# Background copies and additions of weight sums, each behind a finished panel of its own

## The reference, cut to what matters

```
h = layer_norm(ALPHA * h + mix, g, b)
h = layer_norm(ALPHA * h + square(relu(h @ w1)) @ w2, g, b)
```

## Time and profile before

| what | value |
|---|---|
| median of 3 runs | 2704.35 us (2703.06 to 2708.93) |
| profiled execution, its own time | 2705.15 us |
| its span | 2703.2 us |
| PE busy | 2633.5 us, 97% of the span |
| DVE, ACT, POOL busy | 1455.0, 1120.3, 345.0 us |
| moved by SP's queue / by POOL's queue | 260.30 MB / 79.70 MB |

### The profile page before, as it was taken

The page is one execution under the profiler, slowest core; times in us unless marked ns, Lnnn a source line. Parts: engine busy times, 40 slices in busy tenths (PEclk is TensorE's granted clock), DMA queues, the critical chain, the costliest instruction groups (busy, mean ns, idle before and its releaser), DMA issues.

```text
span 2703.2 us, 41070 instructions
## 1 busy us (share of the span) xinstructions
PE 2633.5 (97%) x16968; PEld 2347.4 (87%) x16968; DVE 1455.0 (54%) x2464; ACT 1120.3 (41%) x1833; POOL 345.0 (13%) x414
## 2 busy tenths in 40 slices
PE   8999999999999999999999999999899999999997
PEld 6888999999988888888888988888888897989997
DVE  5664666446543434575556633334666764654655
ACT  4555444334433233353334432322557543433443
POOL 3100310001311000230000410011311130300002
PEclk9999999999999999999999999999999999999998
DMA  9911275335462512256344382252622132233542
GB/s 340 228 51 48 79 285 158 121 114 160 109 149 64 140 63 84 87 188 220 121 142 157 94 238 91 89 147 66 170 86 71 61 104 65 67 105 130 168 141 67
DMA packets 108840, 342.61 MB, mean 127 GB/s; under 512 B 11248, under 2 KB 13680, under 8 KB 108272
## 3 DMA queue, kind: packets, MB, share of 16 engines
q1 hardware_dynamic: 78448, 260.30, 29.3%
q0 software_dynamic: 30208, 79.70, 12.2%
HBM read 337.83 MB, written 81.79 MB: 155 GB/s over the span
## 4 chain that ended last, share of the span: by engine, by line
PE 86%; DVE 4%; ACT 3%; POOL 2%; issue 2%; DMA 2%; SPq 0%; DVEq 0%; POOLq 0%; ACTq 0%
PE ps L693 61%; PE ps L735 14%; PE ps L1040 2%; POOL R L3077 1%; PE ps L1171 1%; PE ps L743 1%; DMA RAW<-in_wf 1%; PE ps L935 1%; PE ps L895 1%; POOL S L3062 1%; PE ps L1026 1%; ACT HT L1445 1%; DVE HT L2186 1%; DVE R L2193 1%; DMA SCR<-in_wfb 1%
## 5 line engine op out<-in xcount | busy, mean ns | idle before, releaser
L2159 DVE TENSOR_TENSOR WL<-RAW,WH 128x1024 fp32r<-128x1024 f32 (+2 forms) x280 | 338.6, 1210 | 249.9 <-ACT WH L1401 248.5
L693 PE MATMUL ps<-HH,LENT 128*128 128x256 f32 (+2 forms) x1848 | 416.1, 321 | 8.8 <-DVE LENT L2159 8.8
L693 PE MATMUL ps<-XH,WH 128*128 128x264 f32 (+2 forms) x1360 | 412.1, 340 | 12.0 <-DVE XL L3036 7.4
L1401 ACT ACTIVATE WH<-RAW 128x1024 fp32r<-128x1024 f32 (+2 forms) x280 | 287.8, 1032 | 279.8 <-PE ps L693 181.8
L693 PE MATMUL ps<-XL,WH 128*128 128x264 f32 (+2 forms) x1360 | 398.7, 331 | 0.0
L693 PE MATMUL ps<-XH,WL 128*128 128x264 f32 (+2 forms) x1360 | 398.0, 330 | 0.0
L2159 DVE TENSOR_TENSOR LENT<-RAW,LENT 128x1024 fp32r<-128x1024 f32 (+2 forms) x220 | 261.2, 1193 | 181.9 <-ACT LENT L1401 180.2
L693 PE MATMUL ps<-XH,LENT 128*128 128x264 f32 (+2 forms) x1392 | 332.6, 328 | 5.3 <-DVE XL L2210 5.1
L693 PEld LDWEIGHTS ps<-HH,LENT 128*128 128x128 f32 x1848 | 302.9, 190 | 36.2 <-DVE LENT L2159 9.9
L1401 ACT ACTIVATE LENT<-RAW 128x1024 fp32r<-128x1024 f32 (+2 forms) x220 | 216.6, 994 | 276.0 <-PE ps L693 169.0
L693 PE MATMUL ps<-HH,WH 128*128 128x512 f32 (+2 forms) x928 | 285.6, 333 | 10.8 <-DVE HL L2252 6.7
(11 more groups left out here) (266 smaller groups left out, 4022.9 us busy)
## 6 DMA issues: line engine op xcount, KB each, us to landing
RAW<-in_wf SPq DMA_DIRECT2D x104, 512.0 KB, 4.3
sum_wf<-in_wf POOLq DMA_DIRECT2D x36, 1024.0 KB, 30.9
RAW<-sum_wf SPq DMA_DIRECT2D x48, 512.0 KB, 3.8
RAW<-in_wr SPq DMA_DIRECT2D x48, 512.0 KB, 3.5
RAW<-in_wg SPq DMA_DIRECT2D x37, 512.0 KB, 3.5
RAW<-in_wu SPq DMA_DIRECT2D x37, 512.0 KB, 4.1
RAW<-in_wd SPq DMA_DIRECT2D x32, 512.0 KB, 3.5
RAW<-in_we SPq DMA_DIRECT2D x24, 512.0 KB, 6.8
```

The lines of the kernel that those rows point to most:

```text
L693: mm = e.matmul(o[:, to:to + m], wt, xt[:, k, c0 + a * m:c0 + (a + 1) * m], start=(n == 0 and j == 0), stop=(n == nk - 1 and j == 2))
L1401: e.activation(slot(u)[0][:, 0:n], raw[:, 0:n], ACT.Copy).then_inc(*S.w_hi(u))
L2159: e.tensor_tensor(lo[:, 0:n], raw[:, 0:n], hi[:, 0:n].bitcast(F32), ALU.subtract).then_inc(*S.w_lo(u))
```

## The change

All 64 background transfers stay as they are, with their sizes. Each now waits for a panel of PE that is its own: a generator hands out places of `PLAN`, and POOL waits for `S.panel` of the next one before it issues the next copy or addition. For MLP 0 these are panels 3 to 26 (`we` 3 to 23 and the first three of `weo`); for MLP 1 the 24 `wf2` panels of chunks 0 to 2 of MLP 0; for the gated MLP the first 16 `wf2` panels of MLP 1. The additions leave the retention, the memory norm and the mixers. The slots and SP's program are untouched.

```diff
+        def sum_copy(key, m):
+            a, h = {"S1": (1, 1), "S3": (0, 0), "S2": (0, 0), "S4": (0, 1)}[m]
+            e.dma_start(sums_of(key)[SUM_AT[m]], quarters(key)[a, h]).then_inc(*S.sum_copy(key, m))
...
+        def sums_beside(panels, keys):
+            for key in keys:
+                for m in ("S1", "S3", "S2", "S4"):
+                    w.wait_ge(*S.panel[final(next(panels))])
+                    sum_copy(key, m)
+            for m in ("S1", "S3", "S2", "S4"):
                 for key in keys:
+                    w.wait_ge(*S.panel[final(next(panels))])
                     sum_add(key, m)
+
+        def downs(layer, chunks):
+            return iter([AT["wf2", 32 * layer + 8 * c + m] for c in chunks for m in range(8)])
...
-        for key in ff_sums[0]:
-            sum_copies(key)
-        sum_adds(ff_sums[0], "S1", "S3", "S2", "S4")
+        sums_beside(iter(range(3, 28)), ff_sums[0])
         down_norm("ln00")
-        for key in ff_sums[1]:
-            sum_copies(key)
+        sums_beside(downs(0, range(3)), ff_sums[1])
         down_norm("ln01")
         for h in range(4):
-            sum_adds(ff_sums[1], *(("S1", "S3"), ("S2",), ("S4",), ())[h])
             for f in range(4):
...
         down_norm("ln10")
-        for key in gu_sums:
-            sum_copies(key)
+        sums_beside(downs(1, range(3)), gu_sums)
         down_norm("ln11")
-        sum_adds(gu_sums, "S1", "S3")
...
         layer_norm("mem", None, 256, lambda k: mem[:, k, :], False)
-        sum_adds(gu_sums, "S2")
         down_norm("ln1")
-        sum_adds(gu_sums, "S4")
```

More of the change, by code:

```diff
@@ L3099, in down_norm, with quarters, sums_of @@
                 layer_norm(ln, half, T // 2, lambda k: R[:, k, c:c + T // 2], dst, {} if half else between)
-        def sum_copies(key):
+        def quarters(key):
             (name, first), n = key, SUM_PAIRS[key]
[L3104 to L3107, removed]
+            return A[name][first:first + 2 * n].rearrange("(q a) p (h k) c -> a h p q (k c)", a=2, h=2)
+        def sums_of(key):
+            return WSUM[key].rearrange("q p s c -> s p q c")
+        def sum_copy(key, m):
+            a, h = {"S1": (1, 1), "S3": (0, 0), "S2": (0, 0), "S4": (0, 1)}[m]
+            e.dma_start(sums_of(key)[SUM_AT[m]], quarters(key)[a, h]).then_inc(*S.sum_copy(key, m))
         def sum_add(key, m):
-            (name, first), n = key, SUM_PAIRS[key]
-            w4 = A[name][first:first + 2 * n].rearrange("(q a) p (h k) c -> a h p q (k c)", a=2, h=2)
-            to = WSUM[key].rearrange("q p s c -> s p q c")
             w.wait_ge(*S.sum_copy[key, m])
@@ L3118, in sum_add @@
                 w.wait_ge(*S.sum_add[key, "S2"])
[L3119 to L3123, removed]
+            more = {"S2": "S1", "S4": "S2"}.get(m)
+            src = sums_of(key)[SUM_AT[more]] if more else quarters(key)[1, 0]
+            e.dma_start(sums_of(key)[SUM_AT[m]], src, accum_op=ALU.add).then_inc(*S.sum_add(key, m))
+        def sums_beside(panels, keys):
[4 more added lines that the diff above has]
+            for m in ("S1", "S3", "S2", "S4"):
                 for key in keys:
+                    w.wait_ge(*S.panel[final(next(panels))])
                     sum_add(key, m)
+        def downs(layer, chunks):
+            return iter([AT["wf2", 32 * layer + 8 * c + m] for c in chunks for m in range(8)])
         ff_sums = [[("wf1", 32 * layer + 8 * c) for c in (1, 2, 3)] for layer in range(2)]
```

## The result

| kernel | median (lowest to highest) | ratio to the kernel before |
|---|---|---|
| before | 2706.30 us (2703.06 to 2708.93), 5 runs | |
| changed | 2717.01 us (2714.32 to 2721.86), 5 runs | 1.0043 [1.0032, 1.0055] |

The forecast was 2704.7 us in a range of 2691 to 2714. The changed kernel is slower by 10.7 us of the medians, or 11.6 by the ratio; the whole interval lies beyond the 0.2% that count as no change. The budget further down is made of these two traces.

A forecast was written before the change was run, and what follows sets the result against it. PE bounds the kernel, busy 97% of the span. Gains of 12.7 us and costs of 13 gave +0.3 us on the profiled 2705.15; with that execution 0.8 above the median, 2704.7 us was predicted, range 2691 to 2714.

The forecast's parts named there:

- which gaps go: Gaps at the start and in the first chunks of MLP 0 and MLP 1 close: 3.5, 4.5 and 4.7 us.
- the three places where that would cost: End of layer 0's attention 5 us, MLP 1's chunk 1 3 us, its chunk 2 4.5 us.
- Rival B: Covers hold at ln00 and the pair stages, about 1 us of costs is left: 2692.7 us; chance 0.26.
- D: POOL's waits are long met when it reaches them, so the bursts stay: 2704.4 us; chance 0.05.
- rival C: MLP 1 chunk 2's pair stage ring-bound at 8.9 us landing; chunk 2 costs 16, chunk 1 5: 2718 us; chance 0.19.
- item 2: End of layer 0's attention: additions in flight slow loads, matmul at ln00 starts 5 us late; bounds 0 and 8.
- 2.5 x 2.4: Ahead of ln00: 2.5 us more per ring turn, between two and three turns, so the split slips 6 us.
- items 4 and 5: MLP 1 pair stages: copies' tail costs chunk 1 3 us (bounds 0, 5), additions cost chunk 2 4.5 (0, 16).
- 7 less 2.7: MLP 1 chunk 1: six units lose 7 us beside copies, less 2.7 of slack; value taken 3.
- `WL` or `LENT`: Sign in the pair stages of MLP 1's chunks 1 and 2: PE's line 735 waits for these of line 2159.
- The rule of the ring: Raw ring of three units: each costs at least (landing + 1.03 ACT + 1.21 DVE + 0.4 hand-over) / 3.
- the slack of 2.7 us: A pair stage first eats about 2.7 us: two units of 2.5 us less one split of 2.3.

The follow-up runs named there:

- the run with empty waits: Changed kernel with MLP 0's copies and additions issued early, POOL still waiting for panels 24 to 26 with nothing to issue: 2708.95 us, ratio 1.0014.
- the shorter one: Changed kernel with a fourth raw buffer from MLP 1 chunk 1's first pair to the end of chunk 2's pairs: 2710.88 us, ratio 1.0013.
- the longer one: Changed kernel with the fourth raw buffer kept through MLP 1 chunk 2's `wf2` panels and chunk 3's pairs: 2706.58 us, ratio 1.0004.

## Why the prediction was wrong

**Right:** what bounds the kernel, which gaps go and about what each gives back (that the sums agree so well, 12.7 and 13.0, is in part luck: 0.9 too much at the start, 0.7 and 0.5 too little in the chunks); that a moved transfer slows the loads at its new place as it did at the old one; the three places where that would cost; and that POOL's waits themselves cost nothing (shown at ln00 by the run with empty waits). Rival B is out (the costs were 23 us), and so is D (the bursts and their waits are gone). What came is the forecast's own mechanism with two of its terms too small, up to the size that rival C gave (2718), though not for C's reason: the loads of chunk 2 landed in 7.0 us, not in 8.9.

**The step that failed first: item 2, ln00, +5 us; measured +10.0.** The forecast had the split of the fifth lead slip by 6 us to 305.4 and the matmul start at 308.3. They came at 305.9 and 308.9, and that this looks close is luck: the forecast's times are on the clock of the trace before, while PE was 2.6 us ahead of it by then, and the chain's first load 2.9 (issued at 276.93 for 279.80). Counted on a clock that starts with PE, the split slipped by 305.9 - (299.43 - 2.6) = 9.1 us and not by 6, and the gap was 8.2 us net and not 5. Two factors of "2.5 x 2.4" were too small. The chain has three turns of the ring, where I took 2.4. And a turn cost 3.2 us more (21.7 - 12.0 = 9.7 us over three), where I took 2.5. The two loads of 10.3 and 11.9 us are not on this chain. That the third turn was as slow as the others has to do with a time that I had too short: I gave each addition 6.5 us and saw the last one land near 300; they landed 9 to 10 us apart, the last at 303.7. The slower clock behind the gap, 1.8 us, was named in the bounds but not in the value, although the same effect was counted among the gains. That the transfers are the cause is shown (without them the gap is absent), and the three slow turns stand in the traces of two more runs (7.7, 7.0 and 7.1 us with only MLP 0 paced; 8.1, 7.0 and 7.3 with the gated additions back). Why additions are slower there than in the earlier trace rows is not shown.

**The second: items 4 and 5, the pair stages, +7.5 us; measured +12.4.** In chunk 2 the price per unit was too low: I took 0.5 us off the landing for half-size units, but they land no sooner beside additions (6.8 to 8.1 us all). The 15 loads came every (1387.7 - 1342.9) / 14 = 3.2 us instead of 3.0, and 16 x (3.2 - 2.5) - 2.7 = 8.5, for 7.6 measured. In chunk 1, five loads landed in 7.2 to 10.6 us, 8.7 on the mean for the 8.4 forecast. My own sum there, 7 less 2.7, gives 4.3; I put it down to 3 because the buffers are full on entry, and it measured 4.8. One sum beside the forecast was wrong too: 3.7 us per unit, in the bound of chunk 2 and in rival C, belongs to a landing of 8.4 us; with 8.9 the rule gives 3.85 and a price of 19 us instead of 16.

**A point that came right by another road.** I expected PE to wait for `WL` or `LENT`. In the stage it waited for line 1489, and just behind it for `HL` of DVE's line 2166 (1.7 us), behind splits of weights that are not due for several us. The rule of the ring gave a fair price all the same, since the order of ACT's and DVE's queues is fixed: a late load delays all that stands behind its split. The two fourth buffers bear it out: with the shorter one the pair stage was whole and PE waited 2.79 us for `HL` behind a late split of a `wf2` panel; with the longer one, which covers those loads, it waited 0.37. How much of the 5.0 us at line 1489 stands behind splits of `wf2` and how much behind splits of the pairs' own units was not separated. It also means that the slack of 2.7 us which I let the stage eat first is no store of ready weights; from this I take it to be how far the splits stand ahead in ACT's queue.

**On the rule of turns between queues.** With the additions in flight across the whole of chunk 2 the loads landed at 7.0 us at the median for 4.0 before, and the DMA engines were busy all the time (share 1.09, 275 GB/s; 0.53 and 162 in the same stage before). From 1356.6 us on at most two additions were in flight or queued at a time, and the ten loads issued from then to 1387.7 us still took 6.8 to 8.1 us, as beside the burst:

```profile
1340.00:1388.00 48.00, 43.04 (x344) 41.49 (x343) 29.26 (x39) 22.45 (x38) 2.16 (x2) 1.00 1.09 275
```

The Trainium skill, "DMA: Bandwidth & Descriptors", section "Queues, rings and completion order", has each DMA engine take turns between the queues that have work. By that rule spreading a burst lowers nothing for the loads that meet it, and the trace agrees (7.0 us at the median, against 6.8 beside the burst).

**Left open:** why ln01 took 1.4 us more than before and ln10 2.1 less, with 0.3 more in the retention between them. It is hardly the change: the runs with only MLP 0 and with only the gated MLP paced have no transfer of POOL's moved in that stretch, and they differ from the trace before by as much at ln01 (1.6 and 1.7 us more) and at ln10 (2.4 and 2.7 less). Open too are the 1.3 us that chunk 2 still lost with the longer fourth buffer.

## What to carry to other kernels

Here a background transfer cost by where it was in flight, not by how many were queued behind it: give it to stretches whose weights come slower than a loaded ring turns (here plain panels at 5.6 us each), and keep it out of stretches where the ring only just keeps up (pair stages at 2.5 us per unit) and away from norms that wait on a queue of splits. When a gain lies ahead of a new gap, put both on one clock: the engine that waits and the chain that it waits for have both moved. Then count the loads on that chain one by one, since each turn pays the whole price. And where splits stand in an in-order queue with the work of the present panels, a late weight for a later panel already holds these.

## What the runs showed of the hardware that was not expected

Three loads issued at 276.9, 278.1 and 279.2 us beside additions landed in 7.6, 10.3 and 11.9 us, where loads issued 3.2 us apart in chunk 2 took 7.0; how much of it they owe to each other was not separated. The 1 MB additions landed 9 to 10 us apart beside the loads there, and 6.5 us apart in the earlier trace rows. A fourth load in flight made all of them later (7.0 to 8.3 us at the median) at a DMA share that was already above 1, yet chunk 2 was nearly whole: with four buffers the sixteen loads from 1338.3 to 1379.5 us came every 2.75 us, with three and the faster landing every 3.2.
